# Hybrid decoder trunk: order of the high and low products in the up projection

## The reference

```
h = rms_norm(x, norm_ffn_pre[l])
u = causal_dwconv(h @ w_up, conv_w) + conv_b        # w_up: 2048 x 11264, 3 taps over time
a, b = split(u, 2)
f = (silu(a) * b) @ w_down                          # w_down: 5632 x 2048
x = x + rms_norm(f, norm_ffn_post[l])
```

## Time and profile before

| what | us |
|---|---|
| median of three runs | 2360.63 |
| the profiled execution | 2362.0 |
| its span, from first to last instruction | 2360.2 |
| TensorE busy with matmuls | 2304.8 |
| VectorE busy | 1617.3 |
| ScalarE busy | 1076.9 |

### The profile page before, as it was taken

The page is one execution under the profiler, slowest core; times in us unless marked ns, Lnnn a source line. Parts: engine busy times, 40 slices in busy tenths (PEclk is TensorE's granted clock), DMA queues, the critical chain, the costliest instruction groups (busy, mean ns, idle before and its releaser), DMA issues.

```text
span 2360.2 us, 36868 instructions
## 1 busy us (share of the span) xinstructions
PE 2304.8 (98%) x13848; PEld 2037.3 (86%) x13848; DVE 1617.3 (69%) x2287; ACT 1076.9 (46%) x1400; POOL 39.5 (2%) x55
## 2 busy tenths in 40 slices
PE   8999999999999999999999999999999999999998
PEld 8999887788888888888899989887888888888886
DVE  5876665787777878555568666557777777785555
ACT  5554444644444444444455444346444444444443
POOL 0000010000000000000000000100000000000000
PEclk9999999999999999999999999999999999999999
DMA  7543334556655655555644424265556556655553
GB/s 239 159 127 108 107 108 158 182 178 194 196 178 186 197 186 198 206 183 196 202 142 145 132 86 140 72 203 165 184 183 198 188 178 195 196 196 197 195 185 136
DMA packets 294790, 401.26 MB, mean 170 GB/s; under 512 B 9256, under 2 KB 269506, under 8 KB 282946
## 3 DMA queue, kind: packets, MB, share of 16 engines
q1 hardware_dynamic: 294420, 400.19, 51.3%
q10 hardware_dynamic: 302, 0.12, 0.0%
HBM read 398.20 MB, written 2.10 MB: 170 GB/s over the span
## 4 chain that ended last, share of the span: by engine, by line
PE 90%; DVE 5%; DVEq 2%; issue 1%; ACT 1%; DMA 0%; ACTq 0%; POOL 0%; POOLq 0%
PE ps L1503 28%; PE ps L1484 14%; PE ps L1485 14%; PE ps L1486 14%; PE ps L1509 14%; PE ps L658 2%; DVE w_lo L1135 2%; PE ps L663 1%; PE ps L709 1%; DVEq L1354 1%; DVEq L1361 0%; PE ps L1555 0%; PE ps L723 0%; DVE x L1181 0%; PE ps L1619 0%
## 5 line engine op out<-in xcount | busy, mean ns | idle before, releaser
L919 ACT ACTIVATE w_hi<-raw 128x1024 fp32r<-128x1024 f32 x740 | 780.2, 1059 | 995.1 <-PE ps L1509 527.5
L1135 DVE TENSOR_TENSOR w_lo<-raw,w_hi 128x1024 fp32r<-128x1024 f32 x744 | 895.6, 1224 | 464.8 <-ACT w_hi L919 457.2
L1503 PE MATMUL ps<-h_both,w_hi 128*128 128x512 f32 x2816 | 888.2, 396 | 4.7 <-DVE h_both L1157 2.9
L1509 PEld LDWEIGHTS ps<-h_both,w_lo 128*128 128x128 f32 x2816 | 530.2, 188 | 124.7
L1509 PE MATMUL ps<-h_both,w_lo 128*128 128x256 f32 x2816 | 555.0, 278 | 0.0
L1503 PEld LDWEIGHTS ps<-h_both,w_hi 128*128 128x128 f32 x2816 | 430.4, 189 | 6.6 <-issue 3.7
L1484 PE MATMUL ps<-w_hi,h_both 128*128 128x512 f32 x960 | 376.1, 392 | 4.2 <-DVE w_lo L1135 4.2
L1486 PE MATMUL ps<-w_hi,h_both 128*128 128x512 f32 x960 | 373.8, 389 | 0.0
L1485 PE MATMUL ps<-w_lo,h_both 128*128 128x512 f32 x960 | 373.6, 389 | 0.0
L1484 PE MATMUL ps<-h_both,w_hi 128*128 128x256 f32 x1216 | 356.5, 293 | 3.4 <-DVE h_both L1157 2.3
L1485 PE MATMUL ps<-h_both,w_hi 128*128 128x256 f32 x1216 | 345.5, 284 | 0.0
(11 more groups left out here) (200 smaller groups left out, 1232.3 us busy)
## 6 DMA issues: line engine op xcount, KB each, us to landing
raw<-in_ffn_w_up SPq DMA_DIRECT2D x88, 2048.0 KB, 8.0
raw<-in_ffn_w_down SPq DMA_DIRECT2D x44, 2048.0 KB, 7.9
raw<-in_w_in SPq DMA_DIRECT2D x37, 2048.0 KB, 8.2
raw<-in_w_out SPq DMA_DIRECT2D x64, 512.0 KB, 5.9
x<-in_x SPq DMA_DIRECT2D x4, 512.0 KB, 7.5
raw<-in_w_in SPq DMA_DIRECT2D x4, 512.0 KB, 8.9
scratch<-in_norm_mix_post SPq DMA_DIRECT2D x2, 1024.0 KB, 10.2
scratch<-in_norm_ffn_post SPq DMA_DIRECT2D x2, 1024.0 KB, 9.9
```

The lines of the kernel that those rows point to most:

```text
L919: act.activation(w_hi[:, s, :], raw_part(l, q, s), ACT.Copy).then_inc(hi_done, 1)
L1135: dve.tensor_tensor(w_lo[:, s, :], raw_part(l, q, s), w_hi[:, s, :].bitcast(F32), ALU.subtract).then_inc(lo_done, 1)
L1503: pe.matmul(ps[:, up_bank(q - P_UP, i), :], w_hi[:, s, c:c + P], h_both[:, k, :, :].rearrange("p a n -> p (a n)"), start=k == 0, stop=Fals ...
L1509: return pe.matmul(ps[:, up_bank(q - P_UP, i), 0:T], w_lo[:, s, c:c + P], h_hi[:, k, :], start=False, stop=True, skip_group_check=True)
```

## The change

In part_up the low products no longer follow the two high products of the same kk. A second loop over kk holds them: first the eight high products of the part (kk = 0 to 3, both tiles), then the eight low ones in the same order. The waits ahead and the signal on the last product stay.

More of the change, by code:

```diff
@@ L1519, in part_up @@
                         up_high(q, s, kk, i)
+                for kk in range(4):
                     for i in range(2):
```

## The result

The changed kernel takes 2367.61 us, the median of 15 runs (2363.90 to 2369.80), against 2362.03 us for the kernel before in its 15 runs (2359.74 to 2365.91). The ratio is 1.0021 with a 95% interval of 1.0014 to 1.0028: slower by about 5 us, where 3.4 us faster was forecast, and outside the forecast's range. One execution of the kernel before (3814.6 us at a mean clock of 0.556) and one of a later variant (3185.4 us at 0.669) were in a slow state and stand in no mean or ratio of this document.

A forecast was written before the change was run, and what follows sets the result against it. TensorE was taken to pace the kernel, with the changed stage about 42% of the run. 344 parts, each 10 ns shorter, save 3.4 us off the median 2360.63, giving 2357.2 us; range 2353.0 to 2361.5 us.

The forecast's parts named there:

- What bounds the stage: Up projection: TensorE paces it, busy nearly throughout at full clock; time is the number of matmuls times start-to-start distance.
- What lies beside: Around the up projection: no new waits; w_lo is ready 2.1 us ahead, and conversions, DMA and PSUM handling stay unaffected.
- What a change of size costs: Gate and up projections: 3.5 to 3.7 ns per trip; one trip a part replaces four, saving 10 ns, 3.4 us overall.
- trip: In the product stream: one change from 512 columns to 256 and back, taken to cost 3.5 to 3.7 ns.
- Does the high run settle: Up projection: whether high-to-high distance falls from 234 to 227 ns in a long run; expected from the third on.
- The handover at 940 us: Up projection's last lows to down projection's 512-column products: two distances of 0.24 and 0.23 us, then eight averaging 0.2275.
- block sum with both ends: One part: eight highs 1.83 us plus eight lows 0.95, together 2.78; saving about nothing to 15 ns, 0 to 5 us.
- Neighbours: Rival, up projection: high-to-high stays 233 ns, low-to-low 115, whatever the run's length; 0.7 us saved, 2359.9 us; chance 0.24.
- Quick lows: Rival, up projection: highs reach 227 ns, lows stay at 115; 43 ns less a part, 14.7 us, 2346 us; chance 0.12.
- The slower rival: Up projection: lows rise to 120 ns, not covering weight loads, highs stay 233; 11.1 us slower, 2371.7 us; chance 0.09.
- The order-free rule: Skill's matmul gap, columns over 2.4 GHz plus about 2.5 ns: 2.600 us a part in any order, so no change.

The follow-up runs named there:

- groups of 4: Four high then four low products, twice in each part of part_up, against the kernel before: ratio 1.0029 (1.0019 to 1.0040), part 2.807 us.

## Why the prediction was wrong

*What bounds the stage* was right: TensorE alone, no wait in the loop, time is starts times distance. *What lies beside* was right as far as waits go: the list of waits didn't change and w_lo was still there 2.1 us ahead (written by 817.30 for a part that starts at 819.49).

*What a change of size costs* is the step that failed. I had one number, 3.5 to 3.7 ns a trip, from two orders that both have very short runs, and took it as a constant that four trips pay four times and one pays once. The runs show a cost that depends on the order, and that is larger in long runs than in runs of two. A trip in runs of two costs 3.3 ns (2786.7 - 2773.3 over four), in runs of four 16.7 (2806.7 - 2773.3 over two), of eight 20.0, and of sixteen still 20.0 for two parts. At eight and more it is the highs' first five distances, together 28 ns above 5 x 226.7, less 8 ns of the first two lows. That two numbers agreed was no evidence for a constant, since both came from one end; and one of them, the gate's, isn't steady: its sixteen couples take from 345 to 356 ns one by one, and the same alternation in the up projection settles at 346.7 or 353.3. One trip of 20.0 in place of four of 3.3 is 6.7 ns a part more, +2.3 us, where I had -3.4.

Kind by kind, the trade looks like this. In the old order the eight highs of a part carry 51.7 ns above 8 x 226.7 and the eight lows 38.3 below 8 x 120, a remainder of 13.3. In the new order it is 27.5 above and 7.5 below, a remainder of 20.0. The change took away half of what the highs paid, as I had hoped, but four fifths of what the lows gave back.

*Does the high run settle* had the warning in it. The handover at 940 us showed settling within two starts, and I took that as the length of the settling. It is no fixed length. In the loop it takes five distances behind eight or sixteen lows. At the handovers to the down projection, one by one in the traces, it takes two behind the two lows of the old order, five behind eight or sixteen, nine behind four, and behind a single low one, seven or ten. The first line is the handover's first start in the changed kernel, the second its sixth; the next two are the first and the tenth with groups of 4:

```profile
942.40 0.40 PE L1484 MATMUL ps<-w_hi,h_both 128*128 128x512 f32 x1
943.56 0.39 PE L1486 MATMUL ps<-w_hi,h_both 128*128 128x512 f32 x1
...
944.62 0.40 PE L1484 MATMUL ps<-w_hi,h_both 128*128 128x512 f32 x1
946.71 0.39 PE L1484 MATMUL ps<-w_hi,h_both 128*128 128x512 f32 x1
```

So the number of lows ahead doesn't set the length by itself; what does is open. In one point the paragraph was right: in the changed kernel the down projection, which streams weights, starts with 233, 236, 228, 233 and 231 ns as the highs do, so h_both isn't the cause. I had also worked out a block sum with both ends, 0 to 15 ns saved, from pieces that each began in other company, and it did not hold what came, a loss. The bound had to be laid below nothing too.

*The rivals.* "Neighbours" came nearest for the part (2784.7 against 2793.3), but its mechanism is wrong: low to low left 115 at once. "Quick lows" is out for that reason. The slower rival had the shape, lows at 120 and highs that stay near 233, and the sign; its size, 32 ns a part, was five times too large, because three of the eight highs do settle and the first lows are quick. I had given it 0.09. Whether weight loads cause it isn't shown: no run changed a load's length.

*The order-free rule.* Five orders of the same 16 products take 2.773 to 2.827 us, so distances don't follow from the columns alone here. The Trainium skill (TensorE: Matmul & The Clock Gate, Back-to-back issue gap) gives the columns over 2.4 GHz plus 2.5 ns for a matmul by itself and says that in a stream with a weight load before each matmul both operations set the spacing. I had left that second part out. This stream is of that kind, so its 226.7 ns in place of the rule's 215.8 don't contradict the rule as it is meant.

*The missing term.* I took the clock as given, since it was 1.00 in the stage. It still is. But about half of the loss, nearly 3 us of 5, isn't in the parts and comes with a lower mean clock. Shown: the old order shifted by 1.1 us loses about as much, the new order in the second layer alone doesn't, and the new order with 2.3 us more work costs no more than the sum of the two. The likeliest reading is that the second layer arrives at another time and loses more to half clock. Not shown: why one arrival should be worse than another on the average over runs, and why the runs of one kernel differ. The profiles give the stretches of one execution per kernel only, and these executions reach the first layer's up projection, ahead of which nothing has changed, at 444.3 to 445.9 us, apart by more than the shift of 1.1 us.

## What to carry to other kernels

When a change only reorders products, don't price a transition from short runs: read the distances one by one after each kind of change and follow them until they stand still, and bound the sum with the longest ramp that the new order can have. A kernel with several half-clock stretches can answer a shift of 1 us with 3 us somewhere else; before a difference of 0.2% is put down to the edit, compare runs at equal mean clock and run the old kernel with a pure delay. An order that alternates sizes had two steady paces here, so one profile of it isn't its time.

## What the runs showed of the hardware that I had not expected

- After a run of eight or sixteen 256-column products, the first five distances of 512-column ones are about 7, 9, 2, 6 and 4 ns above 226.7 ns, the later ones are not; neither the PSUM bank nor the streamed tensor makes a difference. After four it took nine distances to settle, after one from one to ten.
- One instruction sequence, high-low in turn, holds 346.7 ns a couple for one layer and 353.3 for the other in a profiled execution, in one direction in one kernel and in the other in the second.
- Part times of all orders lie on steps of 6.7 ns: 2773.3, 2786.7, 2793.3, 2806.7, 2826.7, and 2 x 2783.3 = 5566.7.
- In means of eleven runs, a shift of the old order by 1.1 us cost 4.1 us (1.7 to 6.1), one by 2.3 us cost 1.3 (-0.7 to 3.5), and one by 3.4 us cost 2.8 (0.5 to 4.5), with the ranges from the ratios' intervals.
